# Block 1 of a two-block transformer kernel: other orders of the ScalarE and VectorE passes at five norms and turns, swapped banks for the memory's transposes, and the first norm's weights on SyncE's queue

## The chip, the cores and the metric

One core of one Trainium2 chip runs the whole program. The metric is the device time of an execution in microseconds, lower is better. Before the change it is 1539.87 us, the median of three runs (1538.3 to 1541.05).

## What is computed

A first block (norm, projection to q, k, v and a pooled branch, differential attention, output projection, cross attention over a memory, gated feed-forward) and then two layers of a second kind (RWKV-like mixing and stick-breaking attention, each between two feed-forwards). The sequence has 256 rows, the width is 1024, everything is float32. The change touches the first block alone:

```python
def first_block(x, mem, ...):
    mem_n = rmsnorm(mem, g_mem)
    h = rmsnorm(x, g_mix_pre)
    proj = h @ w_in
    # q, k with partial rope, v, u = the four parts of proj
    da = diff_attention(q, k, v, lam)
    da = rmsnorm(da, g_subln) * (1.0 - lam_init)
    pooled = causal_multiscale_pool(u)
    po = einsum(pooled, w_pool) * pool_scale
    mix = concatenate([da, po], axis=-1) @ w_out
    x = x + rmsnorm(mix, g_mix_post)
    hq = rmsnorm(x, g_x_pre)
    xq = hq @ w_xq
    kv = mem_n @ w_xkv
    xo = softmax_attention(xq, kv)
    x = x + rmsnorm(xo @ w_xo, g_x_post)
    hf = rmsnorm(x, g_ffn_pre)
    ff = (silu(hf @ w_gate) * (hf @ w_up)) @ w_down
    x = x + rmsnorm(ff, g_ffn_post)
```

## The kernel before

Each float32 product is made of three matmuls on split operands: high times high, high times low, low times high. So every weight goes through four stations. SyncE loads a **unit** of 128x1024 floats (512 KB) into one of four raw slots (`raw`, NR = 4); ScalarE copies it rounded into one of six slots of `wh` (`hi_to`, `more`, line 547); VectorE writes what is left into `wl` (`lo_to`, `more`, line 1103); TensorE multiplies (`x_half`, `w_chunk`, `down`, all through `mm`, line 1763). `load(i)` waits on SyncE for VectorE's `lo` of unit i-4. ScalarE's `hi` of unit i waits for its load and for TensorE's last use of the unit six before it. The units have one fixed order, `plan`: w_in 0 to 15 (four to a chunk of 512 columns), w_xkv 16 to 27, w_out 28 to 35, the last chunk of w_xkv 36 to 39, w_xq 40 to 47, w_xo 48 to 55, mkv 56 and 57, then the first feed-forward from 58 on.

Activations go the same way. A norm of a 128-row half `rb` is a square with a sum on ScalarE (`square_row`, line 557), a scaling on VectorE (`row_mean`, line 1114), a power on GpSimd (`row_power`, line 394) and the product with the weights of the norm on VectorE (`row_norm`, line 1117). TensorE then turns the half by eight 128x128 transposes (`turn`, line 1861) into two banks of PSUM; ScalarE copies the high part out (`turn`, line 554) and VectorE the low part (`turn`, line 1111). The weights of the norms (`gain`) are broadcast to 128 partitions by DMAs on GpSimd's queue; `gb` has two places for them.

All engines run programs written out by hand, one function for each, and each executes its own strictly in order; what stands ahead of a row on an engine holds it up, whoever waits for it. The change speaks of these places, by key:

- "in": the first norm and turn; `gain(0)` is issued by GpSimd, after one memset.
- "mem": the memory's norm and turn (`mh`, `ml`). They fall into the chunks of w_in. TensorE turns half 0 after the second unit of w_in 1024 and half 1 after the third. In w_in 1536 it turns q and k back (`turn_rows`, line 1882) into banks 4 and 5, once after each unit.
- the four heads' `scores(h)` on VectorE: masks (L1111), maxima (L1120), a wait for ScalarE's exponentials, then the reciprocal (L1344) and the weights of the attention. TensorE's `turn_a(h)` (L1999) transposes the weights into bank 4+h.
- "mix" and "q": the norm after w_out is added to `x` (`scale`, `add`), and `x` is normed and turned for w_xq, beside the last chunk of w_xkv (units 36 to 39).
- "xo" and "g0": the same between w_xo and the first feed-forward. `x_lead` does half 0 of the first three units of the feed-forward before half 1 is turned.

The banks and waits of the memory's turn before are these lines:

```python
"mem": (xn, mh, ml, ((6, 7), (4, 5))),
...
for j in x_chunk("w_in", 1536, xh, xl, (2, 3)):
    if j < 2:
        pe.wait_ge(*dve_done.by("T", "mem", 1, j))
    else:
        pe.wait_ge(*act_done.by("qkT", j - 2))
    turn_rows(qk, 2 * j, 4 + j % 2, "qkT", j)
```

Of the kernel before, what the change touches and what calls it, by code (L numbers as in the profile page):

```python
# [14 lines left out]
P = 128  # L15
T = 256
# [110 lines left out]
def build_program(nc, I, cst_in, band_in, out):  # L127
    es = ExitStack()
    with es:
# [6 lines left out]
        gain_in = [sem(f"gain_in{g}") for g in range(2)]  # L136
        id_in, tab_in, mem_in, vec_in, lam_sem, pos_in, band_sem, wpool_in, lora_in, x_out = (
# [169 lines left out]
        gain_by = lambda n: (gain_in[n % 2], 16 * (n // 2 + 1))  # L307
# [4 lines left out]
        TURNS = {"in": (xn, xh, xl, ((2, 3), (4, 5))), "mem": (xn, mh, ml, ((6, 7), (4, 5))),  # L312
# [48 lines left out]
        def sync_program(sp):  # L361
# [6 lines left out]
            sp.dma_start(x[:, 0, :], x_rows[:, 0, :]).then_inc(x_in[0], 16)  # L368
            sp.dma_start(cst[:, 0:P], cst_in[:, 0:P]).then_inc(id_in, 16)
# [14 lines left out]
        def pool_program(pool):  # L384
# [22 lines left out]
            gain(0)  # L407
# [127 lines left out]
        def act_program(act):  # L535
# [14 lines left out]
            def more(n=1):  # L550
                hi_to(split[0] + n)
# [106 lines left out]
            evict("w_in", 512, (2, 3), lambda rb: qk[:, rb, 512:1024], "qk", 1)  # L658
            hi_to(after("w_in", 1024, 1))
            turn("mem", 0)  # L660
            hi_to(after("w_in", 1024, 2))
# [56 lines left out]
            scores(3)  # L718
            hi_to(after("w_xkv", 1024, 1))
            turn_a(2)  # L720
            hi_to(after("w_xkv", 1024, 3))
            turn_a(3)
# [16 lines left out]
            turn("q", 0)  # L739
            act.wait_ge(*dve_done.by("added", "mix", 1, 1))  # L740
            square_row("q", 1, x[:, 1, :], "sq", "q", 0)
            more()
            evict("w_xkv", 1536, (2, 3), lambda rb: vx[:, rb, 512:1024], "vx", 1)
            turn("q", 1)
# [350 lines left out]
        def dve_program(dve):  # L1095
# [220 lines left out]
            for rb in range(2):  # L1316
# [10 lines left out]
                tt(t2, w4[2], w4[3], ALU.add, "rope", rb)  # L1327
            lo_to(after("w_in", 1024, 1))
            turn("mem", 0)
            lo_to(after("w_in", 1024, 2))  # L1330
            turn("mem", 1)

            def scores(h):
# [8 lines left out]
                ts(da_st(h, 1, 0, 0, 4), da_st(h, 0, 0, 0, 4), -sc8, None, ALU.mult, ALU.bypass, "sc_max", h)  # L1342
                dve.wait_ge(*act_done.by("sc", h, 1, 1))
# [12 lines left out]
            scores(0)  # L1356
# [8 lines left out]
            scores(1)  # L1365
            lo_to(after("w_xkv", 512, 2))
            scores(2)
            lo_to(after("w_xkv", 1024, 0))
            scores(3)
# [25 lines left out]
            turn("q", 0)  # L1395
            row_mean("q", 1)
            row_norm("q", 1, x, 3, xn2)
            more()
# [25 lines left out]
            row_mean("g0", 0)  # L1424
            more()
            sum_mean("xo", 1)
            row_norm("g0", 0, x, 5, xn2)
            turn("g0", 0)
            scale("xo", 1, 4, tmp)
            add("xo", 1, tmp)  # L1430
# [1142 lines left out]
```

## Time and profile before

| what | value |
|---|---|
| median of three runs | 1539.87 us (1538.3 to 1541.05) |
| profiled execution, its own time | 1542.03 us |
| its span, first to last instruction | 1540.7 us |
| TensorE matmul busy | 1473.9 us (96%) |
| VectorE busy | 887.5 us (58%) |
| ScalarE busy | 737.7 us (48%) |
| GpSimd busy | 94.2 us (6%) |
| mean granted TensorE clock | 0.985 |
| HBM read | 251.50 MB, 164 GB/s over the span |

All times in the rows below are from one profiled execution and count from the start of its span. PE is TensorE, ACT ScalarE, DVE VectorE, POOL GpSimd, SP SyncE; L557 is line 557 of the kernel. In brackets behind a row stands the idle time of its engine just ahead of it and what ended it. A matmul's end is modelled, so idle times after matmuls are good to about 0.2 us.

### The profile page before, as it was taken

How to read it: one execution, taken by the hardware profiler on the slowest of the kernel's cores; microseconds unless marked ns; L12 is line 12 of the kernel's file. 1: busy time of each engine (PE TensorE's matmuls, PEld its weight loads, DVE VectorE, ACT ScalarE, POOL GpSimd, SP SyncE). 2: the span in 40 equal slices, each digit the busy share in tenths (PEclk: the TensorE clock that was granted, in tenths of full speed). 3: DMA queues.
4: the chain of work that ended last, by engine and by line, in shares of the span. 5: the costliest groups of instructions: out<-in, count | busy, mean ns of one | idle time of the engine just before them, and what ended most of it. 6: DMA issues, size and time to landing. Idle time of an engine off the chain costs nothing.

```text
span 1540.7 us, 23240 instructions
## 1 busy us (share of the span) xinstructions
PE 1473.9 (96%) x9817; PEld 1332.6 (86%) x9817; DVE 887.5 (58%) x1161; ACT 737.7 (48%) x1036; POOL 94.2 (6%) x123
## 2 busy tenths in 40 slices
PE   7899999999999999996999999999999998999997
PEld 5787887999889988996987899889998797789986
DVE  4666656555465556786437655565555665565554
ACT  4654645444354444776213544444444475454442
POOL 3001000000000000001111000000000112300000
PEclk9999999999999999998999999999999999999999
DMA  8644636665666655532002756556656552275652
GB/s 284 224 123 151 233 96 190 181 190 191 178 207 188 189 189 171 185 124 69 1 1 96 232 176 199 192 192 199 186 175 215 170 186 81 69 222 175 203 192 70
DMA packets 121607, 254.06 MB, mean 165 GB/s; under 512 B 8040, under 2 KB 33824, under 8 KB 121248
## 3 DMA queue, kind: packets, MB, share of 16 engines
q1 hardware_dynamic: 117200, 237.07, 49.0%
q0 software_dynamic: 4304, 15.51, 3.2%
q8 instruction: 77, 1.26, 0.3%
q14 instruction: 26, 0.21, 0.0%
HBM read 251.50 MB, written 1.05 MB: 164 GB/s over the span
## 4 chain that ended last, share of the span: by engine, by line
PE 84%; DVE 7%; ACT 5%; DMA 2%; issue 1%; POOL 1%; ACTq 0%; DVEq 0%; POOLq 0%
PE ps L1763 81%; DVE wl L1103 2%; ACT wh L547 1%; DMA raw<-in_w_in 1%; ACT bsa L557 1%; PE ps L1861 1%; DVE xl L1111 1%; PE ps L2198 1%; ACT xh L554 1%; DVE bsw L1111 1%; PE ps L1882 0%; POOL st L394 0%; DMA gb<-in_g_mix_pre 0%; DMA raw<-in_w_xq 0%; ACT junk L557 0%
## 5 line engine op out<-in xcount | busy, mean ns | idle before, releaser
L1103 DVE TENSOR_TENSOR wl<-raw,wh 128x1024 fp32r<-128x1024 f32 x426 | 518.3, 1226 | 421.8 <-ACT wh L547 420.3
L547 ACT ACTIVATE wh<-raw 128x1024 fp32r<-128x1024 f32 x426 | 446.9, 1058 | 435.4 <-PE ps L1763 390.9
L1763 PE MATMUL ps<-xh,wh 128*128 128x256 f32 x1792 | 504.2, 281 | 2.4 <-DVE xl L1111 2.4
L1763 PE MATMUL ps<-xl,wh 128*128 128x256 f32 x1792 | 501.8, 280 | 0.0
L1763 PE MATMUL ps<-xh,wl 128*128 128x256 f32 x1792 | 501.5, 280 | 0.0
L1763 PEld LDWEIGHTS ps<-xh,wh 128*128 128x128 f32 x1792 | 338.3, 189 | 5.5 <-DVE xl L1111 2.9
L1763 PEld LDWEIGHTS ps<-xl,wh 128*128 128x128 f32 x1792 | 338.3, 189 | 0.3
L1763 PEld LDWEIGHTS ps<-xh,wl 128*128 128x128 f32 x1792 | 338.2, 189 | 0.0
L1763 PE MATMUL ps<-wh,fhh 128*128 128x512 f32 x368 | 143.2, 389 | 0.0
L1763 PE MATMUL ps<-wh,fhl 128*128 128x512 f32 x368 | 143.2, 389 | 0.0
L1763 PE MATMUL ps<-wl,fhh 128*128 128x512 f32 x368 | 143.2, 389 | 0.0
L1763 PE MATMUL ps<-wh,xh 128*128 128x512 f32 (+1 forms) x320 | 130.0, 406 | 8.2 <-DVE xl L1111 5.0
L1763 PE MATMUL ps<-wl,xh 128*128 128x512 f32 (+1 forms) x320 | 126.9, 397 | 0.0
L1763 PE MATMUL ps<-wh,xl 128*128 128x512 f32 (+1 forms) x320 | 126.5, 395 | 0.0
L394 POOL TENSOR_TENSOR st<-st,mhalf 128x1 f32<-128x1 f32 (+2 forms) x32 | 22.7, 712 | 1207.2 <-DVE st L1114 1207.1
L1763 PEld LDWEIGHTS ps<-wh,xh 128*128 128x128 f32 x320 | 61.5, 192 | 25.8 <-DVE xl L1111 6.5
L1763 PEld LDWEIGHTS ps<-wh,fhl 128*128 128x128 f32 x368 | 69.1, 188 | 14.3
L1763 PEld LDWEIGHTS ps<-wl,fhh 128*128 128x128 f32 x368 | 69.1, 188 | 14.3
L1763 PEld LDWEIGHTS ps<-wh,fhh 128*128 128x128 f32 x368 | 69.1, 188 | 14.2
L1763 PEld LDWEIGHTS ps<-wh,xl 128*128 128x128 f32 x320 | 61.5, 192 | 14.3
L1763 PEld LDWEIGHTS ps<-wl,xh 128*128 128x128 f32 x320 | 61.5, 192 | 12.7
L554 ACT ACTIVATE fhh<-fhb 128x512 fp32r<-128x512 f32 x45 | 28.5, 633 | 74.4 <-DVE fhb L1111 74.4
(387 smaller groups left out, 1656.7 us busy)
## 6 DMA issues: line engine op xcount, KB each, us to landing
raw<-in_ffn_w_gate SPq DMA_DIRECT2D x88, 512.0 KB, 3.9
raw<-in_ffn_w_up SPq DMA_DIRECT2D x88, 512.0 KB, 3.8
raw<-in_ffn_w_down SPq DMA_DIRECT2D x88, 512.0 KB, 3.5
raw<-in_w_out SPq DMA_DIRECT2D x24, 512.0 KB, 3.4
raw<-in_w_gate SPq DMA_DIRECT2D x22, 512.0 KB, 4.1
raw<-in_w_up SPq DMA_DIRECT2D x22, 512.0 KB, 4.3
raw<-in_w_down SPq DMA_DIRECT2D x22, 512.0 KB, 4.0
raw<-in_rwkv_w_in SPq DMA_DIRECT2D x22, 512.0 KB, 4.5
```

The source lines that it names most:

```text
L394: pool.tensor_tensor(rs, var, mhalf[:, 0:var.free_size()], ALU.pow).then_inc(pool_done.new(("rs", *key)), 1)
L547: act.activation(slot(0, i), raw[:, i % NR, :], ACT.Copy).then_inc(act_done.new(("hi", i)), 1)
L554: act.activation(dst, src, ACT.Copy, scale=scale).then_inc(act_done.new(label), 1)
L557: act.activation(dst, src, f, **how).then_inc(act_done.new(label), 1)
L1103: dve.tensor_tensor(slot(1, i), raw[:, i % NR, :], slot(0, i).bitcast(F32), ALU.subtract).then_inc(dve_done.new(("lo", i)), 1)
L1111: dve.tensor_tensor(o, a, b, op).then_inc(dve_done.new(label), 1)
L1763: return pe.matmul(o, l, r, start=start, stop=stop, skip_group_check=True)
L1861: last = pe.transpose(ps[banks[rb][g]][:, k * P:k * P + P], src[:, rb, c * P:c * P + P], ident)
L2198: last = pe.transpose(bT[:, k * P:k * P + P], XI[:, 4 * g + k, :], ident)
```

## The change

The weights of the first norm come on SyncE's queue, right behind the first half of x, with a semaphore of their own. The banks of the memory's turn are swapped: half 0 now uses 4 and 5. The turning back of q and k waits for half 0, and TensorE waits for half 1 later, ahead of w_xkv. ScalarE and VectorE do the memory's two turns one weight pass (or pair of passes) earlier. VectorE's `scores` is cut into `maxima` and `weights`, and for head 3 two weight passes stand between them and no longer ahead of both; ScalarE's and TensorE's `turn_a` of heads 2 and 3 move ahead of weight passes (TensorE's of head 3 by one unit). At "q" both halves are squared and normed ahead of the low part of half 0's turn, and TensorE's turn of half 1 comes half a unit earlier. At "g0" VectorE norms half 0 ahead of a weight pass, scales half 1 of "xo" ahead of the low part of half 0's turn, and the weight pass follows the addition. No instruction of computing is added or taken away.

```diff
+        first_gain_in = sem("first_gain_in")
...
-        gain_by = lambda n: (gain_in[n % 2], 16 * (n // 2 + 1))
+        gain_by = lambda n: (gain_in[n % 2], 16 * (n // 2 + n % 2)) if n else (first_gain_in, 16)
...
-        TURNS = {"in": (xn, xh, xl, ((2, 3), (4, 5))), "mem": (xn, mh, ml, ((6, 7), (4, 5))),
+        TURNS = {"in": (xn, xh, xl, ((2, 3), (4, 5))), "mem": (xn, mh, ml, ((4, 5), (6, 7))),
...
             sp.dma_start(x[:, 0, :], x_rows[:, 0, :]).then_inc(x_in[0], 16)
+            sp.dma_start(gain_at(0), GAINS[0].partition_broadcast(P)).then_inc(first_gain_in, 16)
             sp.dma_start(cst[:, 0:P], cst_in[:, 0:P]).then_inc(id_in, 16)
...
             pool.memset(mhalf[:, :], -0.5).then_inc(pool_done.new(("half",)), 1)
-            gain(0)
...
             evict("w_in", 512, (2, 3), lambda rb: qk[:, rb, 512:1024], "qk", 1)
+            turn("mem", 0)
             hi_to(after("w_in", 1024, 1))
-            turn("mem", 0)
-            hi_to(after("w_in", 1024, 2))
             turn("mem", 1)
             hi_to(after("w_in", 1024))
...
             scores(3)
+            turn_a(2)
             hi_to(after("w_xkv", 1024, 1))
-            turn_a(2)
+            turn_a(3)
             hi_to(after("w_xkv", 1024, 3))
-            turn_a(3)
...
             square_row("q", 0, x[:, 0, :], "sq", "mix", 1, 1)
-            turn("q", 0)
             act.wait_ge(*dve_done.by("added", "mix", 1, 1))
             square_row("q", 1, x[:, 1, :], "sq", "q", 0)
+            turn("q", 0)
             more()
+            turn("q", 1)
             evict("w_xkv", 1536, (2, 3), lambda rb: vx[:, rb, 512:1024], "vx", 1)
-            turn("q", 1)
...
+            turn("mem", 0)
             lo_to(after("w_in", 1024, 1))
-            turn("mem", 0)
+            turn("mem", 1)
             lo_to(after("w_in", 1024, 2))
-            turn("mem", 1)
...
-            scores(2)
+            maxima(2)
+            weights(2)
+            maxima(3)
             lo_to(after("w_xkv", 1024, 0))
-            scores(3)
+            weights(3)
...
-            turn("q", 0)
             row_mean("q", 1)
             row_norm("q", 1, x, 3, xn2)
+            turn("q", 0)
             more()
             turn("q", 1)
...
             row_mean("g0", 0)
+            row_norm("g0", 0, x, 5, xn2)
+            sum_mean("xo", 1)
+            scale("xo", 1, 4, tmp)
+            turn("g0", 0)
+            add("xo", 1, tmp)
             more()
-            sum_mean("xo", 1)
-            row_norm("g0", 0, x, 5, xn2)
-            turn("g0", 0)
-            scale("xo", 1, 4, tmp)
-            add("xo", 1, tmp)
             row_mean("g0", 1)
...
-                    pe.wait_ge(*dve_done.by("T", "mem", 1, j))
+                    pe.wait_ge(*dve_done.by("T", "mem", 0, j))
...
             pe.wait_ge(*act_done.by("v", 1))
+            pe.wait_ge(*dve_done.by("T", "mem", 1, 1))
             for j in w_chunk("w_xkv", 0, mh, ml, (0, 1)):
...
-                elif j == 3:
+                elif j == 2:
                     pe.wait_ge(*dve_done.by("a", 3, 1))
                     turn_a(3)
...
             x_half("w_xkv", 1536, 3, 0, mh, ml, (2, 3))
-            x_half("w_xkv", 1536, 3, 1, mh, ml, (2, 3))
             pe.wait_ge(*dve_done.by("xn", "q", 1))
             turn("q", 1)
+            x_half("w_xkv", 1536, 3, 1, mh, ml, (2, 3))
             pe.wait_ge(*dve_done.by("T", "q", 1, 1))
```

VectorE at the memory's turn, after the rope (the first row is its last pair); a minus stands in the program before, a plus in the changed one, `wl` is a weight pass, `ml` the low part of a turned half:

```order
 L1111 TENSOR_TENSOR tmp_54<-junk 128x16x8 x2
-L1103 TENSOR_TENSOR wl<-raw,wh 128x1024 x2
 L1111 TENSOR_TENSOR ml<-ps,mh 128x4x128 x2
-L1103 TENSOR_TENSOR wl<-raw,wh 128x1024
+L1103 TENSOR_TENSOR wl<-raw,wh 128x1024 x2
 L1111 TENSOR_TENSOR ml<-ps,mh 128x4x128 x2
-L1103 TENSOR_TENSOR wl<-raw,wh 128x1024 x6
+L1103 TENSOR_TENSOR wl<-raw,wh 128x1024 x7
```

Half 0 no longer has the two weight passes of units 14 and 15 ahead of it, and half 1 stands ahead of that of unit 16.

VectorE at head 3 of the attention, from the end of head 2's weights; the two `tmp_54<-ps,cst` rows are the masks:

```order
 L1114 TENSOR_SCALAR tmp_54<-tmp_54,st 128x256
 L1117 SCALAR_TENSOR_TENSOR tmp_54<-tmp_54,st 128x256
-L1103 TENSOR_TENSOR wl<-raw,wh 128x1024 x2
 L1111 TENSOR_TENSOR tmp_54<-ps,cst 128x384 x2
 L1120 TENSOR_REDUCE st<-tmp_54 128x2 x2
 L1114 TENSOR_SCALAR st<-st 128x4
-L1344 RECIPROCAL st<-st 128x4
+L1103 TENSOR_TENSOR wl<-raw,wh 128x1024 x2
+L1347 RECIPROCAL st<-st 128x4
```

The passes of units 29 and 30 moved from ahead of the masks to between the maxima and the reciprocal.

VectorE between "xo" and "g0"; `xn_64` is the normed half, `tmp_54<-ps,st,gb` the scaling of half 1 of "xo", `xres` the addition:

```order
-L1103 TENSOR_TENSOR wl<-raw,wh 128x1024
+L1117 SCALAR_TENSOR_TENSOR xn_64<-xres,st,gb 128x1024
 L1111 TENSOR_TENSOR st<-st 128x1
 L1114 TENSOR_SCALAR st<-st 128x1
-L1117 SCALAR_TENSOR_TENSOR xn_64<-xres,st,gb 128x1024
-L1111 TENSOR_TENSOR xl<-ps,xh 128x4x128 x2
 L1117 SCALAR_TENSOR_TENSOR tmp_54<-ps,st,gb 128x512 x2
+L1111 TENSOR_TENSOR xl<-ps,xh 128x4x128 x2
 L1111 TENSOR_TENSOR xres<-xres,tmp_54 128x512 x2
+L1103 TENSOR_TENSOR wl<-raw,wh 128x1024
 L1114 TENSOR_SCALAR st<-st 128x1
```

The scaling moved ahead of the turn's low part, and the pass of unit 60 from the top to behind the addition.

## Rows read from the trace of the kernel before

**Rows 1.** The page: busy time by engine; the chain that ended last, by engine.
```profile
PE 1473.9 (96%) x9817; PEld 1332.6 (86%) x9817; DVE 887.5 (58%) x1161; ACT 737.7 (48%) x1036; POOL 94.2 (6%) x123
...
PE 84%; DVE 7%; ACT 5%; DMA 2%; issue 1%; POOL 1%; ACTq 0%; DVEq 0%; POOLq 0%
```

**Rows 2.** Waits of TensorE, 0 to 450 us: us in total, times, longest.
```profile
PE ps L1861 <- DVE xn L1117: 12.5, 3, 9.6
```

**Rows 3.** Timeline of the start, five engines' rows: start, duration, engine, line, operation.
```profile
1.26 0.71 POOL L389 DMA_DIRECT2D gb<-in_g_mix_pre  x1 [0.42 <-issue]
5.83 0.56 POOL L394 TENSOR_TENSOR st<-st,mhalf 128x1 f32<-128x1 f32 x1 [3.86 <-DVE st L1114]
...
8.16 1.28 DVE L1117 SCALAR_TENSOR_TENSOR xn<-xres,st,gb 128x1024 f32<-128x1024 f32 x1 [2.49 <-DMA gb<-in_g_mix_pre]
...
8.88 1.06 ACT L547 ACTIVATE wh<-raw 128x1024 fp32r<-128x1024 f32 x1 [3.39 <-DMA raw<-in_w_in]
...
9.60 1.94 PE L1861 MATMUL ps<-cst,xn 128*128 128x128 f32 x8 [9.60 <-DVE xn L1117]
```

**Rows 4.** Windows: busy of PE, PEld, DVE, ACT, POOL; clock; DMA share; GB/s.
```profile
14.00:15.00 1.00, 1.00 (x3) 0.33 (x1) 0.82 (x1) 1.00 (x2) 1.00 (x3) 1.00 0.53 203
```

**Rows 5.** Timeline at the memory's turn: VectorE, ScalarE and TensorE.
```profile
53.00 2.36 DVE L1103 TENSOR_TENSOR wl<-raw,wh 128x1024 fp32r<-128x1024 f32 x2
55.27 1.28 DVE L1111 TENSOR_TENSOR ml<-ps,mh 128x512 fp32r<-128x512 f32 x2
...
58.12 1.06 ACT L547 ACTIVATE wh<-raw 128x1024 fp32r<-128x1024 f32 x1 [1.09 <-DMA raw<-in_w_xkv]
...
58.34 1.11 PE L1882 MATMUL ps<-cst,tmp 128*128 128x128 f32 x4 [4.52 <-DVE ml L1111]
```

**Rows 6.** The chain's pieces after that wait (start, us), and a window as in rows 4.
```profile
59.46 4.96 PE ps L1763 x12
64.42 0.44 PE ps L1882 x4
64.86 2.79 PE ps L1763 x12
...
58.00:64.00 6.00, 5.66 (x16) 4.59 (x17) 3.15 (x4) 1.65 (x2) 0.00 (x0) 0.50 0.82 249
```

**Rows 7.** Timeline at heads 2 and 3 of the attention: VectorE, then TensorE.
```profile
108.48 1.22 DVE L1103 TENSOR_TENSOR wl<-raw,wh 128x1024 fp32r<-128x1024 f32 x1
...
111.08 1.02 DVE L1111 TENSOR_TENSOR tmp<-ps,cst 128x384 f32<-128x384 f32 x2
...
115.28 0.18 DVE L1344 RECIPROCAL st<-st 128x4 f32<-128x4 f32 x1 [1.93 <-ACT tmp L557]
...
117.06 3.49 DVE L1103 TENSOR_TENSOR wl<-raw,wh 128x1024 fp32r<-128x1024 f32 x3
...
111.68 0.55 PE L1999 MATMUL ps<-cst,tmp 128*128 128x128 f32 x3 [1.01 <-DVE tmp L1111]
...
119.29 2.94 PE L1763 MATMUL ps<-v_sb,aT 128*128 128x128 f32 x24 [1.26 <-ACT aT L554]
```

**Rows 8.** Timeline at "q": VectorE, ScalarE and TensorE.
```profile
150.87 1.29 DVE L1111 TENSOR_TENSOR xres<-xres,tmp 128x512 f32<-128x512 f32 x2
...
155.11 1.07 ACT L557 ACTIVATE junk<-xres 128x1024 f32<-128x1024 f32 x1
...
158.46 1.09 PE L1861 MATMUL ps<-cst,xn 128*128 128x128 f32 x8 [1.18 <-DVE xn L1117]
...
161.12 0.38 PE L1763 MATMUL ps<-xh,wh 128*128 128x256 f32 x1 [1.57 <-DVE xl L1111]
```

**Rows 9.** Timeline at "g0": VectorE and TensorE, and a window as in rows 4.
```profile
234.29 1.40 DVE L1117 SCALAR_TENSOR_TENSOR tmp<-ps,st,gb 128x512 f32<-128x512 f32 x2
...
240.26 1.09 PE L1861 MATMUL ps<-cst,xn 128*128 128x128 f32 x8 [1.71 <-DVE xn L1117]
...
241.60:245.00 3.40, 3.40 (x9) 2.65 (x9) 3.26 (x4) 2.33 (x3) 0.00 (x0) 0.50 0.63 190
```

More of the change, by code:

```diff
@@ L1327, in dve_program, with maxima @@
                 tt(t2, w4[2], w4[3], ALU.add, "rope", rb)
+            turn("mem", 0)
             lo_to(after("w_in", 1024, 1))
-            turn("mem", 0)
+            turn("mem", 1)
             lo_to(after("w_in", 1024, 2))
-            turn("mem", 1)
-            def scores(h):
+            def maxima(h):
                 s = h % 2
@@ L1342, in scores, with weights @@
                 ts(da_st(h, 1, 0, 0, 4), da_st(h, 0, 0, 0, 4), -sc8, None, ALU.mult, ALU.bypass, "sc_max", h)
+            def weights(h):
+                s = h % 2
                 dve.wait_ge(*act_done.by("sc", h, 1, 1))
@@ L1355, in dve_program @@
             lo_to(after("w_xkv", 0, 0))
-            scores(0)
+            maxima(0)
+            weights(0)
             lo_to(after("w_xkv", 0, 3))
@@ L1364, in dve_program @@
             lo_to(after("w_xkv", 512, 0))
-            scores(1)
+            maxima(1)
+            weights(1)
             lo_to(after("w_xkv", 512, 2))
-            scores(2)
+            maxima(2)
+            weights(2)
+            maxima(3)
             lo_to(after("w_xkv", 1024, 0))
-            scores(3)
+            weights(3)
             lo_to(after("w_xkv", 1024, 3))
```

## The prediction

> **What bounds the kernel now.** I read the page first: TensorE is busy in 96% of the span, and 84% of the chain that ended last is TensorE's own work [rows 1]. So time can only be won where TensorE stands still or runs at the low clock. The list of its waits over the first 450 us shows where: the largest class is that for a normed half, 12.5 us in three waits [rows 2]. The timelines of the five places then show who was late, and the windows what clock was granted. In all, TensorE idles at the places that the change touches for 9.60 us [rows 3], 4.52 [rows 5], 1.01 and 1.26 [rows 7], 1.18 and 1.57 [rows 8], and 1.71 [rows 9]. After 245 us nothing is changed, and TensorE's own work carries the chain; what is won in block 1 is passed on to the end, unless the weights cannot follow.
>
> **Start ("in").** The norm's product starts at 8.16 us when its weights land, 2.49 us after VectorE had nothing else to do; the power it also needs is done at 5.83 + 0.56 = 6.39 us [rows 3]. If the weights were there, the product would start at 6.4 and TensorE's first transposes 1.75 us earlier: that is the upper end. But the same queue brings weight unit 0, now behind another 512 KB. ScalarE copies that unit at 8.88 us, ahead of the turned half [rows 3]. By then 1.6 MB had come (x, identity, norm weights, unit 0) in 8.2 us from the first issue, so 512 KB are worth up to 2.6 us; if the unit were pushed back by that, less the 1.75 won, the lower end is -0.8 us. But the bytes ahead of unit 0 are the same as before, they only travelled side by side, so I take it to land about as now. A second limit comes after: the DMA engines are full for most of the first 30 us, and the only slack is around 14 us, at a share of 0.53 [rows 4]; half a microsecond to one can be caught up there, and the margins of the units at TensorE are small. I take **1.2 us**, nearer the upper end. Issue costs: the DMA adds one issue ahead of three others on SP, and takes 0.71 us off POOL [rows 3], all hidden behind full DMA engines.
>
> The Trainium skill, "DMA: Bandwidth & Descriptors", section "Issuing engines are not separate DMA queues", says that DMAs of all issuing engines run on the same 16 DMA engines and interleave, so that the issuer saves only sequencer time. By it this term would be about nothing and the sum 1.2 us smaller. No row here separates order within a queue from sharing between two.
>
> **Memory's turn ("mem").** TensorE waits 4.52 us until 58.34 for the last low part of half 1; it had arrived at 58.34 - 4.52 = 53.82 [rows 5]. VectorE reaches the two weight passes ahead of the turn at 53.00. In the new order the first low part takes their place and is done after 1.28/2 = 0.64 us, at 53.7 [rows 5]. ScalarE's copy is now ahead of its weight passes too. So TensorE hardly waits: **4.5 us**. After the wait the granted clock was 0.50 from 58 to 64 us, that is 1.2 GHz, and twelve matmuls took 4.96 us against 2.79 at 2.4 GHz; four transposes took 1.11 against 0.44 [rows 5, 6]. TensorE had been idle for 4.52 us before it fell; without that it should stay up: 2.17 + 0.67 = **2.8 us**. Given back: the weight passes of units 14 and 15 are 1.28 us later, the load of unit 18 waits for the first of them, and ScalarE already waited for that load until 58.12 [rows 5]. It now comes at about 59.4, one pass (1.06) and one copy (0.6) later, near 61.0, q's and k's first turned part is out of bank 4. TensorE's third turning needs that bank; it comes there at 53.8 + 0.44 + 2.79 + 0.44 + 2.79 = 60.3, so it waits **-0.7 us**. The bound below is that the loads are late by a whole load, some 4 us, which leaves 2.5; above, that nothing is given back, 7.3. Sum of this place: 4.5 + 2.8 - 0.7 = **6.6 us**. The new wait for half 1 ahead of w_xkv is free: its low parts are done 2.36 + 1.28 us after half 0's, near 58, seven microseconds early.
>
> **Head 3.** The masks start at 108.48 where the weight pass stood, not at 111.08 [rows 7], so head 2's turn no longer waits: **1.0 us**. From masks to finished weights it took 117.06 - 111.08 = 6.0 us, including an idle wait for the exponentials of 1.93; two weight passes (2.36) [rows 5, 7] now lie in that wait, so they end at 108.5 + 6.0 + 0.4 = 114.9. But TensorE now wants them one unit earlier, at 111.68 - 1.01 + 0.3 + 2.8 = 113.8 (three transposes, a unit of twelve matmuls): a new wait of **-1.1 us**. After that ScalarE's copy hides behind a whole unit, and the 1.26 us in front of the attention product [rows 7] vanish: **+1.26**. Sum **1.1 us** (from -0.5, if the new wait grows by a pass, to 2.3). The delayed passes are of units 29 and 30, first used after 122 us: hidden.
>
> **"q".** The square of half 1 started at 155.11, behind the copies of half 0, though the sum it reads was complete at 150.87 + 1.29 = 152.16 [rows 8]. From that square to the transposes took 158.46 - 155.11 = 3.35 us, so the normed half is ready at 152.2 + 3.35 = 155.55, and TensorE (done with half a unit at 155.7) turns it at once: the 1.18 us go. Then the low parts bind: VectorE does half 0 (1.28) after 155.5, a weight pass (1.18), half 1 (1.28), to 159.2, against 161.12 now [rows 5, 8]. Sum **1.9 us**; bounds 0.8 (TensorE's wait of 1.18 alone, less rounding) and 2.75, both waits. The weight passes follow 1.2 us earlier, so unit loads are not behind.
>
> **"g0".** VectorE scaled "xo" half 1 from 234.29 for 1.40 us between the turn's low parts and the addition [rows 9]. The scaling now falls into the idle time before the turn, so square, power, product and transposes of half 1 come **1.4 us** earlier; TensorE's wait is 1.71 [rows 9], so it can use that. Unit 60's pass moves behind the addition and ends near 234.3 + 1.3 + 1.2 = 236.8. TensorE ends the three units' half 0 at 240.26 - 1.71 = 238.55 [rows 9] and needs unit 60 for the last 1.4 us of that (half of 2.79), from 237.1: just hidden, and the wait for half 1 covers it if not. Bounds 0.5 to 1.7. Then the clock: after that wait it was 0.50 from 241.6 to 245 us [rows 9], that is 1.2 GHz. By the ratio 2.79/4.96 [rows 6] 3.4 us there hold 1.9 us of work, so **1.5 us** come back if it no longer falls after 0.3 us of idle.
>
> The Trainium skill, "TensorE: Matmul & The Clock Gate", section "Part 1: The HAM clock gate", says that the gate's decisions are free-running against the kernel. By that this 1.5 us is won in some executions only; the trace has one execution and cannot say.
>
> **Sum.** 1.2 + 6.6 + 1.1 + 1.9 + 1.4 + 1.5 = 13.7 us. From the profiled execution's 1542.03 that is 1528.3. The median of the runs shown is 2.2 us lower than the profiled one, part of which may be lows of the clock that other executions did not have, so I take 13.4 off the median: 1539.87 - 13.4 = **1526.5 us**.
>
> **Rivals.** (1) *The start gives nothing*: unit 0 or the units after it arrive no sooner, as full DMA engines speak for; the free share at 14 us speaks against. And the clock at "g0" falls as before. 1539.87 - (13.4 - 1.2 - 1.5) = 1529.2. (2) *The memory's wait moves instead of going*: unit 18's load or the copies of q and k come a whole load late, TensorE stands 3 to 4 us at the third turning, and the clock falls there. The place then gives about 1.5 instead of 6.6: 1531.6. For it speaks that ScalarE already waits for that load; against, that twelve matmuls lie between every two turnings. (3) *The change gives more*: the start 1.75, nothing given back at "mem", 0.3 more at "g0": 1526.5 - 1.6 = 1524.9, less if lows elsewhere go. (4) *Slower*: many short waits in place of one long one keep TensorE at 1.2 GHz through the memory's products, from 54 us on. Each microsecond of full-speed work then costs 4.96/2.79 - 1 = 0.78 us more. 13.4 us are eaten after 17 us of such work, about 31 us at the low clock; with 40 us, 17.5 are lost: 1544. Against it: waits of 1.0 and 1.26 us [rows 7] or 1.18 and 1.57 [rows 8] had no low window after them.
>
> **Chances.** Forecast 0.58, (1) 0.17, (2) 0.10, (3) 0.12, (4) 0.03. A measurement of this kernel can tell about 0.2%, 3.1 us, from no change. All but (4) lie beyond it, though some of (2) may end near: faster 0.94, same 0.03, slower 0.03. The range leaves out (4) and the far part of (2): 1522 to 1531.5.
>
> **What would show it.** Right: transposes of "in" from about 8 us; no wait over 0.3 us at 52 to 54, one of about 0.7 at the third turning and no clock of 0.50 between 50 and 70; a wait of about 1.1 ahead of head 3's turn and none ahead of the attention product; the first w_xq product about 1 us after the last of w_xkv; a wait under 0.5 us before "g0" half 1. Wrong: the first 0.50 window returns after the memory's turn, a wait for a weight pass shows up on TensorE between 20 and 60 us, or the gain at 245 us is not there at the end.

## The result, and the profile after

| | before | changed |
|---|---|---|
| median, measured side by side | 1539.86 us (1538.3 to 1541.05, 4 runs) | 1527.68 us (1526.4 to 1529.7, 4 runs) |
| second pair, later | 1540.55 us (1535.84 to 1544.2, 11 runs) | 1526.49 us (1526.01 to 1529.72, 6 runs) |
| profiled execution, its span | 1542.03, 1540.7 us | 1526.75, 1525.3 us |
| mean granted TensorE clock | 0.985 | 0.990 |

The ratio is 0.9919 with a 95% interval of 0.9906 to 0.9933, and 0.9911 (0.9895 to 0.9927) in the second pair. The kernel is faster by 12.2 and 14.1 us; the forecast of 1526.5 lies between the two medians.

The page of the changed kernel answers to [rows 1], its chain by engine behind it:

```profile
PE 1466.5 (96%) x9817; PEld 1328.4 (87%) x9817; DVE 887.4 (58%) x1161; ACT 737.3 (48%) x1036; POOL 92.6 (6%) x122
...
PE 86%; DVE 7%; ACT 4%; DMA 1%; issue 1%; POOL 0%; SPq 0%; ACTq 0%; DVEq 0%
```

The span is 15.4 us shorter, but TensorE's busy time fell by only 7.4 us, at the same 9817 matmuls. In this pair of executions, then, some 8 us are waits that went, and 7.4 us are matmuls that ran at 2.4 instead of 1.2 GHz. Not all of that comes from the change: up to the 1400th matmul the busy time fell by 5.1 us (249.3 to 244.2) of the 14.6 us won there, and the other 2.3 us lie in stages that it doesn't touch.

Where it was won is best seen by giving each matmul its number in TensorE's order, which is the same in both kernels at these points, and subtracting its two start times:

| point | before | changed | lead | predicted part |
|---|---|---|---|---|
| before the memory's turn | 52.02 | 51.52 | 0.50 | start 1.2 |
| behind its four turnings | 71.27 | 63.39 | 7.89 | "mem" 6.6 |
| behind the attention product's start | 125.11 | 115.79 | 9.32 | head 3: 1.1 |
| first w_xq product | 161.12 | 149.74 | 11.38 | "q" 1.9 |
| "g0", half 0 | 231.76 | 220.08 | 11.68 | |
| behind "g0", half 1 | 241.40 | 228.35 | 13.05 | "g0" 1.4 |
| some 30 us on | 272.56 | 257.97 | 14.59 | its clock 1.5 |
| 600 | 599.99 | 585.41 | 14.58 | |
| 850 | 849.95 | 835.92 | 14.03 | |
| 1500 | 1499.92 | 1484.55 | 15.37 | |

Everything up to 14.59 is won in block 1, and it is still there at the end. The later steps of -0.5 and +1.3 are in stages that the change doesn't touch; for the second, the clock stood at 1.2 GHz for 6.8 us near 1293 in the profile of before, and for 3.4 us near 1279 in this one.

**Start.** SyncE's, VectorE's, ScalarE's and TensorE's rows of the timeline of the changed kernel, against [rows 3]:

```profile
1.17 0.42 SPq L370 DMA_DIRECT2D gb<-in_g_mix_pre  x1
...
6.77 1.28 DVE L1117 SCALAR_TENSOR_TENSOR xn<-xres,st,gb 128x1024 f32<-128x1024 f32 x1 [1.12 <-DMA gb<-in_g_mix_pre]
9.94 1.23 DVE L1103 TENSOR_TENSOR wl<-raw,wh 128x1024 fp32r<-128x1024 f32 x1 [1.88 <-ACT wh L548]
...
8.85 1.06 ACT L548 ACTIVATE wh<-raw 128x1024 fp32r<-128x1024 f32 x1 [3.39 <-DMA raw<-in_w_in]
...
8.20 1.94 PE L1868 MATMUL ps<-cst,xn 128*128 128x128 f32 x8 [8.20 <-DVE xn L1117]
11.91 0.77 PE L1770 MATMUL ps<-wh,xh 128*128 128x512 f32 x1 [1.77 <-DVE xl L1111]
```

The norm's product starts at 6.77 instead of 8.16, the transposes at 8.20 instead of 9.60. But TensorE then waits 1.77 us, and its first product is at 11.91, where it had been at 12.19. Weight unit 0 is the limit: ScalarE copies it at 8.85 (8.88 before), VectorE makes its low part at 9.94, and only then the low part of x.

**Memory's turn.** The timeline of VectorE, then TensorE, against [rows 5, 6]:

```profile
51.18 1.28 DVE L1111 TENSOR_TENSOR ml<-ps,mh 128x512 fp32r<-128x512 f32 x2
52.38 2.35 DVE L1103 TENSOR_TENSOR wl<-raw,wh 128x1024 fp32r<-128x1024 f32 x2
54.64 1.28 DVE L1111 TENSOR_TENSOR ml<-ps,mh 128x512 fp32r<-128x512 f32 x2
...
53.15 0.60 PE L1889 MATMUL ps<-cst,tmp 128*128 128x128 f32 x4
56.38 0.60 PE L1889 MATMUL ps<-cst,tmp 128*128 128x128 f32 x4
59.60 0.60 PE L1889 MATMUL ps<-cst,tmp 128*128 128x128 f32 x4
62.83 0.60 PE L1889 MATMUL ps<-cst,tmp 128*128 128x128 f32 x4
```

The window from 50 to 70 us of the same trace, with its columns as in [rows 4]:

```profile
50.00:70.00 20.00, 20.00 (x123) 17.13 (x122) 15.15 (x21) 14.56 (x20) 0.00 (x0) 1.00 0.67 226
```

TensorE is busy for all 20 us, at a clock of 1.00. The four turnings of q and k stand without a wait; even the third, to which I had given 0.7 us.

**Head 3.** VectorE's masks, weight passes and reciprocal, then TensorE, against [rows 7]:

```profile
100.58 1.02 DVE L1111 TENSOR_TENSOR tmp<-ps,cst 128x384 f32<-128x384 f32 x2
...
102.76 2.35 DVE L1103 TENSOR_TENSOR wl<-raw,wh 128x1024 fp32r<-128x1024 f32 x2
105.03 0.17 DVE L1347 RECIPROCAL st<-st 128x4 f32<-128x4 f32 x1
...
106.95 0.55 PE L2006 MATMUL ps<-cst,tmp 128*128 128x128 f32 x3 [1.07 <-DVE tmp L1117]
```

The reciprocal starts without idle time, since the two passes fill the 1.93 us in which VectorE had waited. The waits of 1.01 and 1.26 are gone, and the one of 1.07 is new.

**"q" and "g0".** ScalarE's square of half 1 and TensorE's two rows at "q"; then VectorE's scaling and TensorE's turn at "g0", in the timeline, against [rows 8, 9]:

```profile
142.87 1.06 ACT L558 ACTIVATE junk<-xres 128x1024 f32<-128x1024 f32 x1 [4.08 <-DVE xres L1111]
...
146.44 1.03 PE L1868 MATMUL ps<-cst,xn 128*128 128x128 f32 x8
149.74 0.39 PE L1770 MATMUL ps<-xh,wh 128*128 128x256 f32 x1 [0.87 <-DVE xl L1111]
...
219.66 1.41 DVE L1117 SCALAR_TENSOR_TENSOR tmp<-ps,st,gb 128x512 f32<-128x512 f32 x2 [0.66 <-POOL st L396]
...
227.21 1.09 PE L1868 MATMUL ps<-cst,xn 128*128 128x128 f32 x8 [0.42 <-DVE xn L1117]
```

The window over most of block 1:

```profile
20.00:300.00 280.00, 274.11 (x1706) 242.20 (x1705) 174.94 (x259) 153.00 (x244) 15.28 (x26) 1.00 0.59 186
```

The square now starts when the sum is there, the turn of half 1 has no wait, and of 1.57 us ahead of w_xq 0.87 are left; at "g0" 0.42 of 1.71. From 20 to 300 us the clock is 1.00 throughout.

### The profile page after: what moved, and what is told of

Read it like the earlier page. It is cut to its first block, busy times and chain, and to the rows that moved or that the text cites. A ratio compares the mean times of both kernels' runs of the same rounds, so it can differ in the third digit from the quotient of the medians.

```text
span 1525.3 us, 23240 instructions
## 1 busy us (share of the span) xinstructions
PE 1466.5 (96%) x9817; PEld 1328.4 (87%) x9817; DVE 887.4 (58%) x1161; ACT 737.3 (48%) x1036; POOL 92.6 (6%) x122
## 3 DMA queue, kind: packets, MB, share of 16 engines
q8 instruction: 77, 1.26, 0.3%
## 4 chain that ended last, share of the span: by engine, by line
PE 86%; DVE 7%; ACT 4%; DMA 1%; issue 1%; POOL 0%; SPq 0%; ACTq 0%; DVEq 0%
PE ps L1770 84%; DVE wl L1103 2%; ACT wh L548 1%; PE ps L1868 1%; ACT bsa L558 1%; DVE xl L1111 1%; PE ps L2206 1%; DVE st L1120 1%; DVE bsw L1111 1%; PE ps L1889 0%; DMA raw<-in_w_in 0%; ACT xh L555 0%; DMA raw<-in_w_xo 0%; DVE xres L1173 0%; POOL st L396 0%
```

## The experiments

My theory was the sum of the prediction. The rivals: the start gives nothing; the gain at "mem" is mostly the turn's banks and not the order of passes; the clock's part is luck, so that single parts don't add up. Each part was first made alone in the kernel before; then parts were taken out of the changed kernel.

**Only the start.**

```diff
+            sp.dma_start(gain_at(0), GAINS[0].partition_broadcast(P)).then_inc(first_gain_in, 16)
             sp.dma_start(cst[:, 0:P], cst_in[:, 0:P]).then_inc(id_in, 16)
...
-            gain(0)
```

> The kernel before with only the start changed (the first norm's weights on SyncE's queue). Theory: what binds is weight unit 0, which lands at 8.85 us as before; TensorE's first product comes 0.3 us earlier, and TensorE reaches the memory's turn 0.5 us earlier, but waits there for VectorE, whose chain is ahead by more (1.3 to 1.8 us), because the later loads land sooner. Then the time falls by 1.3 to 1.8 us, ratio about 0.999. Rival (a uniform shift of TensorE's program): 0.3 to 0.5 us less, ratio 0.9997.

Measured: 1538.81 us (12 runs) against 1540.11 (35 runs), ratio 0.9993 (0.9983 to 1.0003). The 1.3 us are what the theory said, but the interval includes no change and the rival's 0.3 to 0.5. TensorE's waits in its timeline:

```profile
7.95 1.94 PE L1862 MATMUL ps<-cst,xn 128*128 128x128 f32 x8 [7.95 <-DVE xn L1118]
12.02 0.76 PE L1764 MATMUL ps<-wh,xh 128*128 128x512 f32 x1 [2.13 <-DVE xl L1112]
...
56.60 0.66 PE L1883 MATMUL ps<-cst,tmp 128*128 128x128 f32 x4 [3.18 <-DVE ml L1112]
```

The window after the last of them:

```profile
57.50:60.90 3.40, 3.40 (x9) 2.65 (x9) 1.91 (x2) 0.39 (x1) 0.00 (x0) 0.50 0.81 249
```

The transposes come earlier, the first product doesn't. The unchanged wait at the memory's turn is 3.18 us here, with 3.4 us of low clock, not 4.52 and 6.8 as in the profile of before. At "q" and "g0", unchanged too, the clock didn't fall.

**Only the memory's turn** (banks, orders of ScalarE and VectorE, TensorE's waits).

```diff
-"mem": (xn, mh, ml, ((6, 7), (4, 5))),
+"mem": (xn, mh, ml, ((4, 5), (6, 7))),
...
+            turn("mem", 0)
             lo_to(after("w_in", 1024, 1))
-            turn("mem", 0)
+            turn("mem", 1)
             lo_to(after("w_in", 1024, 2))
-            turn("mem", 1)
```

> The kernel before with only the memory's turn changed (banks, waits, the orders of ScalarE's and VectorE's passes there). Theory: the wait of 4.5 us and the low clock of 2.8 us after it go, and without the changed start VectorE is not ahead, so TensorE waits about 0.7 us at the third turning of q and k: 6.6 us less, ratio 0.9957. Rival (this place is independent of the start): no such wait, 7.3 us less, ratio 0.9953. If the low clock comes back although the wait is gone: 4.5 us, 0.997.

Measured: 1535.93 us (12 runs), ratio 0.9975 (0.9965 to 0.9986). Two waits of TensorE that the kernel before did not have, in the timeline:

```profile
38.52 0.50 PE L1762 MATMUL ps<-wh,xh 128*128 128x512 f32 x1 [0.74 <-ACT tmp L554]
62.08 0.66 PE L1881 MATMUL ps<-cst,tmp 128*128 128x128 f32 x4 [0.92 <-ACT qkT L554]
```

Two windows at "q" and "g0" in the same trace:

```profile
155.30:158.70 3.40, 2.96 (x14) 2.96 (x15) 3.26 (x4) 2.39 (x3) 0.00 (x0) 0.50 0.93 337
237.20:240.60 3.40, 3.40 (x9) 2.62 (x8) 3.26 (x4) 2.20 (x3) 0.00 (x0) 0.50 0.64 172
```

Of the predicted 6.6 us 4.2 came, with an interval of 2.2 to 5.4, so the term was too high. The long wait and its low clock are gone. The third turning does wait, 0.92 us, as foretold, and at "q" the clock fell, which it had not done in the profile of before with the same two waits.

**Only head 3.**

```diff
-            scores(2)
+            maxima(2)
+            weights(2)
+            maxima(3)
             lo_to(after("w_xkv", 1024, 0))
-            scores(3)
+            weights(3)
```

> The kernel before with only the attention's part changed (masks of head 3 ahead of two weight passes, the turns of heads 2 and 3). Theory: the waits of 1.01 and 1.26 us ahead of head 2's turn and of the attention product go, a new one of about 1.1 us stands ahead of head 3's turn: 1.1 to 1.4 us less, ratio 0.9992. Rival: the waits of block 1 are not on the path that sets the end: 0.

Measured: 1539.95 us (12 runs), ratio 0.9998 (0.9989 to 1.0007). Its trace has the new wait, 1.07 us at 113.07, and neither the 1.26 nor the 1.01. Three of its windows, at "q", "g0" and in an unchanged stage:

```profile
157.60:161.00 3.40, 3.09 (x14) 3.09 (x15) 3.26 (x4) 2.26 (x3) 0.00 (x0) 0.51 0.95 328
239.60:243.00 3.40, 3.40 (x10) 2.63 (x9) 3.25 (x4) 2.06 (x3) 0.00 (x0) 0.50 0.56 161
700.40:717.50 17.10, 7.44 (x29) 5.48 (x28) 11.81 (x30) 13.90 (x38) 0.00 (x0) 0.50 0.11 33
```

The local step is right, but 1.1 us can't be seen in the times: the bound of that interval is 1.7 us below no change.

**Only "q".**

```diff
-            turn("q", 0)
             row_mean("q", 1)
             row_norm("q", 1, x, 3, xn2)
+            turn("q", 0)
```

with the same on ScalarE, and TensorE's turn of half 1 half a unit earlier.

> The kernel before with only the norm and turn 'q' changed. Theory: TensorE starts w_xq 2.0 us earlier, the wait ahead of it falls from 1.18 + 1.57 to about 0.9, and the chain of loads, ScalarE and VectorE behind it is ahead too, so all of it is kept: 2.0 us less, ratio 0.9987. Rival (the loads of w_xq bind ScalarE's copies of the queries): a wait of 1 to 2 us appears ahead of the first scores of the cross attention, and 0 to 1 us is left.

Measured: 1537.0 us (12 runs), ratio 0.9982 (0.9973 to 0.9992). TensorE's timeline at "q":

```profile
157.66 0.39 PE L1763 MATMUL ps<-xh,wh 128*128 128x256 f32 x1 [0.86 <-DVE xl L1111]
```

The wait is the 0.87 of the changed kernel. The 3.1 us are more than the 1.9 of the waits. The traces have the rest: from the first w_xq product to the 216th matmul behind it, it took 28.6 to 28.9 us in the three kernels with the old "q" and a low window there, 27.8 and 28.0 in the two without one, and 27.3 here. The two without one lost part of it in waits of 0.22 and 0.40 us for ScalarE's copy of the queries. Beside this kernel the five lost 1.1 us on average, and 1.9 + 1.1 is close to the 3.1 measured. No trace of a changed "q" has a low window.

**Only "g0".**

```diff
-            more()
-            sum_mean("xo", 1)
             row_norm("g0", 0, x, 5, xn2)
-            turn("g0", 0)
+            sum_mean("xo", 1)
             scale("xo", 1, 4, tmp)
+            turn("g0", 0)
             add("xo", 1, tmp)
+            more()
```

> The kernel before with only VectorE's order at 'g0' changed. Theory: the wait ahead of half 1's turn falls from 1.71 to 0.4 us and the granted clock stays at 1.0 behind it: 1.5 + 1.5 = 3.0 us less, ratio 0.998. Rival (the clock falls there in some executions only, or its fall moves elsewhere): 1.5 us less, ratio 0.999, and lows of the clock in other stretches.

Measured: 1538.08 us (11 runs) against 1539.85 (15 runs), ratio 0.999 (0.998 to 1.0). The 1.8 us are nearer to the rival's 1.5, and the interval of 0 to 3.1 includes the theory's 3.0 as well as no change. The wait is 0.41 us and no low window follows; at "q", unchanged here, there is one, in this window:

```profile
159.10:162.50 3.40, 3.40 (x18) 3.40 (x18) 3.06 (x3) 1.42 (x2) 0.00 (x0) 0.51 0.90 325
```

The five parts alone give 1.3 + 4.2 + 0.2 + 3.1 + 1.8 = 10.6 us, each good to about 1.5; the change gave 12.2 and 14.1. That they add up is within the intervals. The traces show that the start and the memory's turn are not quite independent; the numbers stand below, with the run that puts the first weights back.

**The changed kernel without the memory's part.**

```diff
-"mem": (xn, mh, ml, ((4, 5), (6, 7))),
+"mem": (xn, mh, ml, ((6, 7), (4, 5))),
```

with the orders of all three engines as before.

> The changed kernel without the memory's part. Theory (start and memory's part depend on each other): the wait ahead of the first turning is about 3.3 us (4.5 + 0.5 - 1.8) and the clock falls after it, so the time is that of before less 1.5 + 1.4 + 2.0 + 1.5 (+1.5 for the clock at 'g0'), 6.4 to 7.9 us. Rival (places add up independently as read in the changed kernel's trace, 7.4 for the memory): 12.2 - 7.4 = 4.8 us less than before.

Measured: 1532.83 us (5 runs), ratio 0.9954 (0.9941 to 0.9968). That is 7.0 us less than before, as the theory said, and the rival's 4.8 lies just outside the interval of 4.9 to 9.1. TensorE at the memory's turn:

```profile
56.50 0.66 PE L1890 MATMUL ps<-cst,tmp 128*128 128x128 f32 x4 [3.47 <-DVE ml L1112]
```

This part is worth 0.0035 to 0.0043 of 1540 us, 5.4 to 6.6 us. The traces say 4.9: the 400th matmul starts at 89.5 against 84.6, that is the wait of 3.47 and 1.4 for 3.4 us of low clock.

**The changed kernel with the banks swapped, but ScalarE's and VectorE's orders at "mem" as before.**

```diff
-            turn("mem", 0)
             lo_to(after("w_in", 1024, 1))
-            turn("mem", 1)
+            turn("mem", 0)
             lo_to(after("w_in", 1024, 2))
+            turn("mem", 1)
```

> The changed kernel with ScalarE's and VectorE's orders at the memory's turn as before (banks and waits stay changed). Theory: the low part of half 0 is again behind the two weight passes, 2.3 us later, so TensorE waits some 1.5 to 2.3 us ahead of the first turning; the wait is too short for the clock to fall: 1.5 to 2.3 us more than the changed kernel. Rival (the banks and waits give everything, the passes are hidden): no wait, same time. Second rival (the clock falls): 3 to 4 us more.

Measured: 1528.0 us (6 runs), ratio 0.9917 (0.99 to 0.9934). TensorE's first turning, in its timeline:

```profile
54.72 0.66 PE L1890 MATMUL ps<-cst,tmp 128*128 128x128 f32 x4 [1.49 <-DVE ml L1112]
```

The wait is 1.49 us and the clock stayed up. So of the 4.9 us the banks (and the waits that go with them), put in first, give 3.47 - 1.49 = 2.0 and the 1.4 of clock, and the orders the 1.5 that are left. The orders without the banks were not run, so what they would give alone is open. The times of the whole can't tell 1.5 us: 0.9917 against 0.9911, from the same runs of before.

**The changed kernel with the first weights back on GpSimd's queue.**

```diff
-            sp.dma_start(gain_at(0), GAINS[0].partition_broadcast(P)).then_inc(first_gain_in, 16)
...
+            gain(0)
```

> The changed kernel with the first norm's weights back on GpSimd's queue. Theory (the start is worth more through the lead that it gives to VectorE's and ScalarE's chain than at the start itself): TensorE's first product 0.3 us later, and a wait of 0.7 to 0.9 us for the copy of the turned q and k, perhaps one of 0.7 near 38 us, as in the kernel with the memory's part alone: 1.3 to 1.9 us more than the changed kernel. Rival: only the 0.3 to 0.5 us of the start itself.

Measured: 1528.43 us (6 runs), ratio 0.9918 (0.9903 to 0.9933), beside 1526.49 us and 0.9911 for the whole change. The 1.9 us by the medians and 1.1 by the ratios are on the theory's side, but the intervals overlap. From the timeline, VectorE's product, ScalarE's first copy, and TensorE:

```profile
8.80 1.28 DVE L1116 SCALAR_TENSOR_TENSOR xn<-xres,st,gb 128x1024 f32<-128x1024 f32 x1 [3.11 <-DMA gb<-in_g_mix_pre]
...
9.44 1.06 ACT L547 ACTIVATE wh<-raw 128x1024 fp32r<-128x1024 f32 x1 [3.93 <-DMA raw<-in_w_in]
...
12.82 0.76 PE L1769 MATMUL ps<-wh,xh 128*128 128x512 f32 x1 [0.65 <-DVE xl L1110]
...
61.48 0.66 PE L1888 MATMUL ps<-cst,tmp 128*128 128x128 f32 x4 [0.55 <-ACT qkT L554]
```

In this execution both loads were late, the first product 0.9 us and the 1400th matmul 1.6 us (261.6 against 260.0). That is one sample at the edge: over all traces the first product is at 11.72 to 12.82 with the weights on GpSimd's queue (six) and at 11.55 to 12.02 on SyncE's behind x (seven), with medians of 11.83 and 11.84.

At the first product nothing is won, then. Behind it something is. TensorE in the kernel before waits once more, for the low part of unit 1:

```profile
15.46 0.80 PE L1763 MATMUL ps<-wh,xh 128*128 128x512 f32 x1 [0.38 <-DVE wl L1103]
```

and VectorE's pass for that unit stands here in the changed kernel, at 14.18 in the one before:

```profile
12.89 1.23 DVE L1103 TENSOR_TENSOR wl<-raw,wh 128x1024 fp32r<-128x1024 f32 x1 [0.47 <-ACT wh L548]
```

All six kernels with the norm's weights on GpSimd's queue have this wait of 0.38 us, and none of the seven; the pass starts at 13.71 to 14.82 us in the six and at 12.62 to 13.00 in the seven. The last matmul ahead of the memory's turn starts at 53.9 us in the six and at 52.9 in the seven, by the medians; the scatter within each group is 0.6 to 1.2 us, part of it because the clock first rose at 15.3 to 17.8 us. For the 400th matmul the traces give, as medians with the number of kernels:

| memory's turn | weights on GpSimd's queue | on SyncE's | start's gain |
|---|---|---|---|
| old order | 90.9 (4) | 89.6 (2) | 1.3 |
| new order | 86.8 (2) | 84.8 (4) | 2.0 |

**The changed kernel with unit 0 issued ahead of the norm's weights.**

```diff
-            sp.dma_start(gain_at(0), GAINS[0].partition_broadcast(P)).then_inc(first_gain_in, 16)
             sp.dma_start(cst[:, 0:P], cst_in[:, 0:P]).then_inc(id_in, 16)
             load(0)
+            sp.dma_start(gain_at(0), GAINS[0].partition_broadcast(P)).then_inc(first_gain_in, 16)
```

> The changed kernel with the first norm's weights issued behind weight unit 0 instead of ahead of it. Theory (unit 0's landing binds the start): unit 0 lands about 1 us earlier, near 7.6, and the norm's weights at about the time of the kernel before; ScalarE's copy of unit 0 no longer holds up the turned half, but the norm is at 8.2 again, so the first product moves from 11.91 by no more than 0.3 us either way. Rival (DMA order matters): the start is later by 1.3 us and the time rises by 1.3 us against the changed kernel.

Measured: 1529.04 us (5 runs), ratio 0.9931 (0.9919 to 0.9944). The same three engines' rows of its timeline:

```profile
8.81 1.28 DVE L1117 SCALAR_TENSOR_TENSOR xn<-xres,st,gb 128x1024 f32<-128x1024 f32 x1 [3.13 <-DMA gb<-in_g_mix_pre]
...
7.31 1.06 ACT L548 ACTIVATE wh<-raw 128x1024 fp32r<-128x1024 f32 x1 [1.81 <-DMA raw<-in_w_in]
...
12.84 0.77 PE L1770 MATMUL ps<-wh,xh 128*128 128x512 f32 x1 [0.65 <-DVE xl L1111]
```

Unit 0 comes 1.5 us earlier, the norm's weights 2.0 us later, and the first product 0.9 us later, where the theory allowed 0.3. The 1400th matmul is only 0.4 us later than in the changed kernel (260.5 against 260.0), so the 2 to 3 us by the times lie mostly behind block 1. The order within one queue decides which of the two waits is paid; neither order avoids both.

**The changed kernel with TensorE's turn of head 3 back behind unit 27.**

```diff
-                elif j == 2:
+                elif j == 3:
```

> The changed kernel with TensorE's turn of head 3 put back behind unit 27. Theory: the wait of 1.07 us ahead of it is due to this move alone; it goes, and about 0.3 us for ScalarE's copy appears ahead of the attention product: 0.7 us less than the changed kernel. Rival: the copy's wait of 1.26 us returns in full and the time is that of the changed kernel or 0.2 us more.

Measured: 1526.08 us (1525.47 to 1526.71, 4 runs), ratio 0.991 (0.9896 to 0.9924). TensorE at the attention product, in its timeline:

```profile
110.04 2.94 PE L1770 MATMUL ps<-v_sb,aT 128*128 128x128 f32 x24 [0.58 <-ACT aT L555]
```

The new wait of 1.07 goes, and 0.58 comes back ahead of the attention product: 0.5 us less, which the times can't tell from nothing. This execution also has, ahead of that place, a wait at the third turning that the changed kernel's two traces don't have, and its 1400th matmul starts at 260.05 us, as there:

```profile
60.10 0.66 PE L1889 MATMUL ps<-cst,tmp 128*128 128x128 f32 x4 [0.56 <-ACT qkT L555]
```

**Further than the change:** the last one, and unit 40's pass moved into idle time at "q", a copy moved ahead of "g0"'s turn, and VectorE's addition put between the two low halves there. VectorE's part:

```diff
+            more()
             row_mean("q", 1)
...
-            turn("g0", 0)
+            turn_half("g0", 0, 0)
             add("xo", 1, tmp)
+            turn_half("g0", 0, 1)
```

> The changed kernel taken further: TensorE's turn of head 3 back behind unit 27; at 'q' the weight pass of unit 40 moves into the idle time ahead of the square on ScalarE and behind the addition on VectorE; at 'g0' mk2 is copied ahead of the turned half, and VectorE puts the addition between the two low parts of half 0. Theory (each remaining wait is ended by the pass that is moved): the wait of 0.87 us ahead of w_xq goes, 0.5 us is saved at head 3 and 0.65 at 'g0': 2.0 us less than the changed kernel. Rival (another operand comes last at these places): the waits change their releaser, and less than 0.7 us is won.

Measured: 1527.54 us (6 runs), ratio 0.9916 (0.9901 to 0.9932). The 1400th matmul starts at 258.8 instead of 260.0, so block 1 is 1.2 us shorter. The wait ahead of w_xq is gone and head 3 gave 0.5, as expected, but "g0" only 0.18 where 0.65 was expected (waits of 1.12 and 0.35 instead of 1.23 and 0.42). The gain isn't there at the end, and one reason is a window in an unchanged stage, where the changed kernel had 3.4 us at 1.2 GHz:

```profile
641.60:648.40 6.80, 6.80 (x33) 6.70 (x33) 5.73 (x7) 4.23 (x6) 2.66 (x1) 0.50 0.29 94
```

**The changed kernel again,** unchanged, as a second sample.

> The changed kernel itself, beside the three others, as their yardstick and for a second sample of where the granted clock falls. Theory (the clock's lows in block 1 are gone with the waits): no stretch of 0.50 between 20 and 600 us again, time 1527 to 1528.5. Rival (they fall by chance there): at least one such stretch.

Measured: 1526.49 us (6 runs), ratio 0.9911 (0.9895 to 0.9927). TensorE at head 3 in it:

```profile
107.23 0.55 PE L2006 MATMUL ps<-cst,tmp 128*128 128x128 f32 x3 [1.06 <-DVE tmp L1117]
```

The waits at head 3, "q" and "g0" repeat within 0.1 us (1.06, 0.85, 1.23, 0.41), one ahead of the cross attention's scores doesn't (0.30 against 0.64), and again no low clock falls between 20 and 600 us. No version beat the changed kernel by an amount that the times can tell.

## Why the prediction was right, and where its terms were not

**Sign, size and range** held: 1526.5 against 1527.68 and 1526.49. The sum against the profiled execution was 13.7, and the same two executions differ by 15.28, of which 14.6 in block 1. It fell close partly because errors cancelled, as the last point but one shows.

**Start, 1.2 us: about the right size, but not on the path that I costed.** The step that failed is that I costed the transposes and let the first product follow. The row of ScalarE's copy of unit 0 at 8.88 stood in [rows 3], and behind it lie a weight low part and the turned low parts, up to 11.9. I used that row for a delay of the load only, not as a limit that was already there. At the first product 0.28 us were won in the two profiles, and over all traces nothing. What was won instead came through VectorE's and ScalarE's passes behind it: 1.0 us ahead of the memory's turn, 1.3 and 2.0 at the 400th matmul with the old and the new turn. The times (1.3 us alone, 1.1 to 1.9 taken out of the change) agree, but can't tell this from nothing. So rival (1) was right on unit 0, and the traces speak against it on the units after it; with two to seven profiles on a side, the size is good to about 1 us.

The Trainium skill, "DMA: Bandwidth & Descriptors", "Issuing engines are not separate DMA queues", says that another issuing engine saves only sequencer time. By it the term would have been nothing, and at the first product it was. For a single early load the traces differ: the norm's product started at 6.38 to 6.85 us in the seven traces with SyncE's queue right behind x, and at 7.70 to 8.80 in the six with GpSimd's. That is more than the 0.71 us of GpSimd's issue.

**"mem", 6.6 us.** The lead grew by 7.39 in the two profiles: the wait of 4.52 and 2.87 for the clock, against 4.5 and 2.8. The clock fell at 57.3 us, when TensorE had waited for 3.5 us, and not after the whole 4.52 as I had written. The third term, -0.7, was a size that depends on the execution. Its mechanism is shown: ScalarE's copy for q and k follows the weight pass of unit 18, and ends some 1.55 us after that pass starts. The pass started at 57.21, 57.82 and 57.86 in three kernels with the whole start's part, and no turning waited; at 58.50 in a fourth (head 3 put back), with a wait of 0.56, since TensorE itself was there 1.4 us earlier than without the start's part; at 59.89 without the start's part, with 0.55; at 60.48 with the memory's part alone, with 0.92. Most of the difference between the groups is already there in VectorE's pass of unit 14, which frees the slot for that load: it starts at 52.38 to 52.85 in the four and at 53.91 and 54.94 in the two. What the load itself adds differs by up to 1.2 us from one execution to the next, and why was not found. And the profile of before overstated the place: the same wait measured 3.18, 3.38, 3.76, 3.63 and 3.47 in five other kernels that keep it, with 3.4 us of low clock in each and not 6.8. A typical value of the place is 3.5 + 1.4 = 4.9 us; the 5.4 to 6.6 by the times are each good to about 2 us and don't speak against it. Rival (2) fell: with the new order no wait over 1 us took the old one's place.

**Head 3, 1.1 us** (-1.1 predicted and 1.07 measured for the new wait, the two old ones gone): the lead grew by 1.43, of which the waits are 1.01 + 1.26 - 1.07 = 1.20.

**"q", 1.9 us:** the lead grew by 2.06, the waits by 1.18 + 1.57 - 0.87 = 1.88. What the term missed is the clock. In five kernels that keep the old "q", the traces have a low window there in three (only "mem", only head 3, only "g0") and in two not (before, only the start). With it and the short waits for the queries behind it, the old "q" cost 1.1 us more than its two waits, on average of the five. I had taken the one profile without a low window as evidence against a fall after short waits, in rival (4) too.

**"g0", 1.4 and 1.5 us:** 1.37 and 1.54 measured. The old wait is 1.71 us, and was followed by a low window in three of five kernels that keep it; after the new one, none in the traces of the changed kernel and its variants. So the clock's term is right where it is spent, and is an average of less in many executions. The Trainium skill, "TensorE: Matmul & The Clock Gate", "Part 1: The HAM clock gate", says that the gate runs free against the kernel and does not start anew with it. The runs are in line with that: the same wait, a fall in three of five. At 1.5 us in three of five, "g0" has about 0.9 to win by the clock where I took 1.5.

**The median.** The profiled execution of before was 2.2 us above its median. I put that down to lows that others didn't have, and only 0.3 of it in block 1; by the other traces 2.5 us were at the memory's turn alone (4.52 + 2.87 against 4.9). With typical values the start and the memory's turn together are 90.9 - 84.8 = 6.1 us at the 400th matmul, and the sum is 6.1 + 1.2 + 1.9 + 1.1 + 1.4 + 0.9 = 12.6 us, where I took 13.4; the times gave 12.2 and 14.1, good to about 2 and 2.5. So the two clock terms that I took too high (2.8 against 1.4, 1.5 against 0.9) and the one at "q" that I took at nothing cancelled in part, and that the forecast fell between the two medians is partly luck. If the true gain lies above 12.6, the rest is in the stages behind: from the 1400th matmul to the last it took 1256.9 and 1256.2 us in the two profiles of the changed kernel, and 1257.6 to 1258.4 in the six of the kernel before and its single parts. Whether the change brings that or chance does stays open; the variants that end between 1256.8 and 1258.8 speak for chance.

**Rival (4)** fell: from 20 to 300 us the clock was 1.00 in all of the window, with short waits in it.

## What to carry to other kernels

When an early load is hastened, follow the path past the first instruction that gains to the first one that needs something else: here the transposes moved by 1.4 us and the first product by 0.3. Then look further down too: the passes behind it had moved, and some 1.0 us were there 40 us later. When an engine waits because two results share a bank of PSUM, try to swap the banks before you reorder the passes of other engines: here the swap, put in first, brought 3.4 us of 4.9. And a wait of TensorE costs its length plus a chance of 1.5 us of low clock, so take its price from several profiles, and prove a step of under 2 us by its own rows, since the time of the whole can't.

## What the runs showed of the chip that I had not expected

- A stretch of 3.4 us at 1.2 GHz costs about 1.5 us of TensorE's work (1.54 at "g0"; 1.4 at the memory's turn; 1.3 to 1.6 at "q"). One came with the waits of 3.18 to 4.52 us in all six traces that have them, those of 1.2 to 1.7 us at "q" and "g0" in six cases of ten, and not with the one of 1.49 at the memory's turn, nor with any of 1.0 to 1.3 at head 3.
- The stages behind block 1, which no kernel here changed, took 1256.2 to 1258.8 us in the fourteen profiles, with 23.9 to 34.1 us of low clock in them. That hid the 1.2 us of the version that went further: it took 1258.6.
- The order of two loads in one queue moved each by 1.5 to 2.0 us, and the choice of the queue for the norm's weights moved their use by 0.9 to 2.4, though the same bytes are loaded.
